# Routing of a mixture of experts rewritten: sums of squares, top two, ranks and block numbers computed in another way

## The chip, the cores and the metric

One core of a Trainium2 chip runs the whole program. The metric is the device time of one execution in microseconds. The core has five engines that run side by side and meet at semaphores: TensorE (matrix products, PE in the profile), VectorE (DVE), ScalarE (ACT), GpSimd (POOL) and SyncE (SP, which here only issues DMAs). Sixteen DMA engines move data between the main memory and the on-chip memory.

## The reference

One layer of a streaming encoder on 544 tokens (512 of a prompt and 32 of a sample), 1024 wide. After the two mixers comes `x = x + merged @ w_out`, and then the part that the change is about:

```python
h2 = rmsnorm(x)
g_prob = softmax(h2 @ w_rg + b_rg)                    # 4 groups
p_top, g_top = top_k(g_prob, 1)
e_logits = (h2 @ w_re + b_re).reshape(n, 4, 8)        # 32 experts
v_top, i_top = top_k(e_logits[arange(n), g_top], 2)
gates = softmax(v_top) * p_top
...                                                   # the tokens are sorted by expert
y[tok] += gate * (silu(xb @ w_gate[e]) * (xb @ w_up[e])) @ w_down[e]
```

Each token goes to two experts of one group. An expert has three weight matrices of 2 MB each in fp32, 192 MB over all.

## The kernel before

All products run in fp32 or in two fp32r parts. The tokens lie in five tiles, four of 128 and one of 32. In the last product of the mixers, "W_o", the result comes out with features on partitions: 8 tiles `yT[:, j, :]` of 128 features by 544 tokens. They are made in a loop over j on TensorE (`product("wo", j)`), ScalarE copies each out of the accumulators, and TensorE adds the tile's part of the router's logits behind the next product (`logits(j)`, L1274, out 64 x 544).

After the last tile TensorE turns the five token tiles back to tokens on partitions (`x2_rows`, L1296), and the logits too (L1304). ScalarE takes squares with a running sum (L1763), a root over all (L1767, which first loads a function table), VectorE copies the rows (L2090) and takes the inverse. Then ScalarE scales the rows into `h2` (L1773) and SyncE stores them to main memory (L777, `rows_stored`).

VectorE does the routing, each step waiting for the one before it (`run` = instruction, then wait): logits scaled and biased (L2100, L2104), the group's maximum and its one-hot (`first_max`, four instructions), all experts outside of the group pushed down, then the largest, its one-hot, the second and its one-hot (L2132 to L2143). `chosen` lets TensorE count with two fp32 products how many earlier tokens chose each expert (L1312, L1313). VectorE sums the totals over the tiles (L2156), finds by comparisons and a scan of five doublings how many blocks of 64 slots each expert needs (L2159 to L2166), the slot of each choice (to L2178), its block by 47 comparisons (L2189, L2190), and one-hots of block and lane (L2192 to L2197), with GpSimd making a part of them (L902, L904). Twenty-five bf16 products turn these into token numbers by slot (L1320 to L1323, `maps_done`). Every expert has one block of 64 slots of its own; overflow blocks are handled in a loop behind the thirtieth expert, that runs only if there are any (`n_more`).

With the first 128 numbers (`gidx`, L2217) GpSimd gathers the rows of the first pair of experts from main memory (L889), TensorE turns them (L1374), VectorE scales them (L2246) and the expert loop begins: up products (L1348, L1350), SiLU and gate, down products (L1364, L1365), a scatter of the results, the next gather. Ahead of it, TensorE spreads the gates of the last two experts over partitions (L1337) and VectorE builds two selection matrices from them (L2233).

The experts' weights lie in three places of three parts each. SyncE issues the loads in a fixed order (`load_expert`, L764): the first two experts' parts but one behind the mixers' last weights, the third's first part after W_o, then the five stores of `h2`, then the second's last part after all rows are turned, and the third's two other parts after `rows_stored`. From there on a part is loaded when the products have read what lies in its place.

Of the kernel before, what the change touches and what calls it, by code (L numbers as in the profile page):

```python
# [20 lines left out]
ALU = mybir.AluOpType  # L21
# [8 lines left out]
P = 128  # L30
# [26 lines left out]

COLS = {}
# [9 lines left out]
for _name, _n in (("ident", P), ("tri16", P), ("causal", P), ("before", P), ("rope", TOK), ("iota4", GROUPS),  # L68
                  ("iota32", NE), ("base", NE), ("steps", 8), ("blocks", NOVER), ("valid", NT), ("lane", P), ("iota_blk", NBLK), ("blk_start", NBLK - 1), ("tok_p", NT), ("tok_i", NT),
                  ("half", 1)):  # L70
    CONST_AT[_name] = (_c, _n)
    _c += _n
# [3 lines left out]
def shape_constants():  # L76
# [20 lines left out]
    put("iota32", np.arange(NE) - 64.0)  # L97
    put("base", np.arange(NE) * float(SLOTS))
    put("steps", np.arange(1, 9) * float(SLOTS))
    put("blocks", np.arange(NOVER) * 1.0)  # L100
    valid = np.ones((P, NT), np.float32)
    valid[DEC:, NT - 1] = 0.0
    put("valid", valid)
    put("lane", r[None, :] % SLOTS)
    put("iota_blk", np.arange(NBLK) * 1.0)
    put("blk_start", np.arange(1, NBLK) * float(SLOTS))
    put("tok_p", (r[:, None] + 1) * valid)
    put("tok_i", np.arange(NT) * float(P) * valid)
    put("half", (r[:, None] >= SLOTS) - 4.0)
# [165 lines left out]
def _build(nc, t, ctx):  # L275
# [30 lines left out]
    khigh = R("khigh", [1, P], BF16)  # L306
    g_mix = R("g_mix", [P, KD])
# [99 lines left out]
    ob_hi = N_("ob_hi", [P, 8, TOK], F32R)  # L407
    sg1 = N_("sg1", [P, TOK])
# [23 lines left out]
    lgT = F_("lgT", [64, TOK])  # L432
# [18 lines left out]
    over_blk = M_("over_blk", [P, 2 * NT, NBLK - 1])  # L451
    is_blk = M_("is_blk", [P, 2 * NT, NBLK])
    q_p = M_("q_p", [P, 2 * NT, NBLK], BF16)
    q_i = M_("q_i", [P, 2 * NT, NBLK], BF16)
    q_c = M_("q_c", [P, NT, NBLK], BF16)
    lanes = M_("lanes", [P, 2 * NT, P], BF16)
    vacant = M_("vacant", [P, NBLK])
# [109 lines left out]
    logits_done = sem("logits_done")  # L567
    lgT_copied = sem("lgT_copied")
# [3 lines left out]
    x2_ready = sem("x2_ready")  # L572
# [8 lines left out]
    blk_ready = sem("blk_ready")  # L581
    onehots_i_ready = sem("onehots_i_ready")
# [57 lines left out]
    r5 = [T_(f"r5_{n}", [P, NT])[:, :] for n in range(4)]  # L640
# [3 lines left out]
    rE = T_("rE", [P, NT, NE])[:, :, :]  # L644
    rT = T_("rT", [P, NT, NE])[:, :, :]
    O1 = T_("O1", [P, NT, NE])[:, :, :]
    O2 = T_("O2", [P, NT, NE])[:, :, :]
    picks = T_("picks", [P, NT, NE])
    rank = T_("rank", [P, NT, NE])[:, :, :]
    base = T_("tile_base", [P, NT + 1, NE])  # L650
    rd = T_("rd", [P, NT])[:, :]
    cum = [T_(f"cum{n}", [P, NE])[:, :] for n in range(2)]
    nb = T_("nb", [P, NE])[:, :]
    nb8 = T_("nb8", [P, NE, 8])[:, :, :]
    nbe = T_("nbe", [1, NOVER, NE])[:, :, :]
    bef = T_("bef", [1, NOVER])[:, :]
# [6 lines left out]
    assert U_.at <= T_.at  # L663
# [184 lines left out]
    def _(pool):  # L848
# [51 lines left out]
        pool.wait_ge(blk_ready, 1)  # L900
        for c in range(2):
            nc.gpsimd.tensor_tensor(q_i[:, c * NT:(c + 1) * NT, :], is_blk[:, c * NT:(c + 1) * NT, :],  # L902
                                    con("tok_i").unsqueeze(2).to_broadcast([P, NT, NBLK]), ALU.mult)
        nc.gpsimd.tensor_tensor(q_c[:, :, :], is_blk[:, NT:, :], con("valid").unsqueeze(2).to_broadcast([P, NT, NBLK]),  # L904
                                ALU.mult).then_inc(onehots_i_ready, 1)
# [49 lines left out]
    def _(pe):  # L955
# [313 lines left out]

        def logits(j):  # L1270

            pe.wait_ge(x2T_read, j + 1)
            for half in range(2):
                mm = pe.matmul(bank[0:64, 2 + half, 0:HALF], w_rt[:, j, :], yT[:, j, half * HALF:(half + 1) * HALF],  # L1274
                               start=(j == 0), stop=(j == KD - 1))
            if j == KD - 1:
                mm.then_inc(logits_done, 1)

        for j in range(8):
            product("wo", j)  # L1280
            if j >= 1:
                logits(j - 1)
        logits(7)

        def x2_rows(i):

            r = ROWS[i]
            if i in (0, 3):
                if i:
                    pe.wait_ge(x2_ready, 1)  # L1290
# [8 lines left out]
        for i in range(3):  # L1299
            x2_rows(i)  # L1300
        pe.wait_ge(lgT_copied, 1)
        for i in range(NT):
            r = ROWS[i]
            mm = pe.transpose(bank[0:r, 2, i * 64:(i + 1) * 64], lgT[:, i * P:i * P + r], ident[0:64, 0:64])  # L1304
        mm.then_inc(lg_done, 1)
        for i in range(3, NT):
            x2_rows(i)

        pe.wait_ge(chosen, 1)
        pe.wait_ge(x2_ready, NT)  # L1310
        Mf = picks[:, :, :].rearrange("p i e -> p (i e)")
        pe.matmul(bank[:, 0, 0:NT * NE], con("before"), Mf, start=True, stop=True)  # L1312
        pe.matmul(bank[:, 1, 0:NT * NE], ones[:, :], Mf, start=True, stop=True).then_inc(ranks_done, 1)  # L1313

        pe.wait_ge(onehots_ready, 2)
        pe.wait_ge(onehots_i_ready, 1)
        at = bank[:, 3, 0:NBLK]
        for n in range(2 * NT):
            pe.matmul(at, lanes[:, n, :], q_p[:, n, :], start=(n == 0), stop=False)  # L1320
            mm = pe.matmul(at, lanes[:, n, :], q_i[:, n, :], start=False, stop=(n == 2 * NT - 1))
        for i in range(NT):
            mm = pe.matmul(bank[:, 2, 0:NBLK], lanes[:, NT + i, :], q_c[:, i, :], start=(i == 0), stop=(i == NT - 1))  # L1323
        mm.then_inc(maps_done, 1)
# [4 lines left out]
        pe.wait_ge(gidx_ready, 1)  # L1329
# [3 lines left out]
        for s in range(2):  # L1333
            row = proj[:, s, :, :].rearrange("p a b -> p (a b)")
            for i in range(NT):
                r = ROWS[i]
                mm = pe.matmul(row[:, i * P:i * P + r], last_gates[0:r, i, s:s + 1].to_broadcast([r, P]), ident[0:r, 0:r],  # L1337
                               start=True, stop=True)
# [60 lines left out]

        turn_rows(16)  # L1400
# [95 lines left out]
    def _(act):  # L1496
# [255 lines left out]
        for j in range(8):  # L1752
# [4 lines left out]
        act.wait_ge(logits_done, 1)  # L1757
        nc.scalar.copy(halves(lgT[:, :]), bank[0:64, 2:4, 0:HALF]).then_inc(lgT_copied, 1)

        for i in range(NT):  # L1760
            r = ROWS[i]
            act.wait_ge(x2_turned, i + 1)
            step(nc.scalar.activation(h2[0:r, i, :].rearrange("p (a b) -> p a b", a=2), x2_source(i)[0:r], ACT.Square,  # L1763
                                      accum_out=st_x[0:r, 1, i:i + 1]))
            step.settle()
            act.sem_inc(x2_squared, 1)
        nc.scalar.activation(st_x[:, 1, :], st_x[:, 1, :], ACT.Sqrt, scale=1.0 / D, bias=eps_col[:, :]).then_inc(x2_rms, 1)  # L1767
        act.wait_ge(x2_inv, 1)
        for i in range(NT):

            r = ROWS[i]
            act.wait_ge(x2_ready, i + 1)
            nc.scalar.mul(h2[0:r, i, :], X[0:r, i, :], st_x[0:r, 4, i:i + 1]).then_inc(h2_ready, 1)  # L1773
# [608 lines left out]
```

## Time and profile before

| what | us |
|---|---|
| median of 3 runs (1191.23 to 1192.43) | 1191.29 |
| the profiled execution | 1190.86 |
| its span in the profile | 1189.0 |
| TensorE busy | 1031.5 |
| VectorE busy | 380.1 |
| ScalarE busy | 281.7 |
| GpSimd busy | 238.7 |

The busy times are sums over the span, and tell nothing of which engine is waited for at a given moment; the last 430 us and the 50 us ahead of them are quite different stages.
### The profile page before, as it was taken

What the parts mean: (1) busy time and instruction counts of PE and PEld (TensorE: products, weight loads), DVE (VectorE), ACT (ScalarE), POOL (GpSimd) and SP (SyncE); (2) the same over time, 40 slices, a digit from 0 to 9 for tenths busy, and PEclk for the clock granted to TensorE, in tenths of its full rate; (3) what the DMA queues carried; (4) which work ended last, traced back from release to release, by engine and by line L of the source; (5) the groups of instructions that cost most, each with busy time, mean ns of one, the idle gap of its engine ahead of it and who ended that gap; (6) DMA issues with size and microseconds to landing.
All of it is one profiled execution on the core that took longest, in us unless ns stands there. A gap on an engine that the chain in (4) does not pass through costs nothing.

```text
span 1189.0 us, 15070 instructions
## 1 busy us (share of the span) xinstructions
PE 1031.5 (87%) x6236; PEld 709.2 (60%) x6236; DVE 380.1 (32%) x715; ACT 281.7 (24%) x449; POOL 238.7 (20%) x134
## 2 busy tenths in 40 slices
PE   3987999999989998999999279998888778888886
PEld 2976787776978887999998143333333333233332
DVE  6067322334357419332100821211111111111117
ACT  5234434336254524222211500000000000000003
POOL 3322112121321226433421011111111100111100
PEclk9988999998999979999999679998888998888898
DMA  7335111110321122343355739999999999999994
GB/s 203 77 89 190 36 36 41 50 36 19 98 54 28 45 63 68 92 130 110 90 226 220 322 115 411 428 427 429 432 429 429 433 429 429 432 429 429 427 416 156
DMA packets 109470, 267.60 MB, mean 225 GB/s; under 512 B 22477, under 2 KB 89325, under 8 KB 96194
## 3 DMA queue, kind: packets, MB, share of 16 engines
q1 hardware_dynamic: 104706, 258.11, 56.2%
q0 software_dynamic: 4704, 8.64, 1.9%
q8 instruction: 45, 0.74, 0.3%
q14 instruction: 15, 0.12, 0.0%
HBM read 256.17 MB, written 18.17 MB: 231 GB/s over the span
## 4 chain that ended last, share of the span: by engine, by line
PE 58%; DMA 24%; DVE 11%; issue 3%; ACT 3%; SPq 0%; DVEq 0%; ACTq 0%
PE proj L999 29%; DMA we<-in_w_exp_up 22%; PE proj L1348 11%; PE proj L1364 3%; PE bank L1091 2%; PE bank L1121 2%; DMA raw<-in_w_in 1%; DVE ors L1829 1%; PE proj L975 1%; PE bank L1108 1%; DVE ex L1994 1%; PE bank L1374 1%; PE bank L1274 1%; PE proj L1237 1%; DVE ex L1977 1%
## 5 line engine op out<-in xcount | busy, mean ns | idle before, releaser
L1348 PE MATMUL proj<-we,xsT 128*64 128x512 f32 x512 | 251.8, 649 | 65.5 <-DMA we<-in_w_exp_up 55.2
L1350 PE MATMUL proj<-we,xsT 128*64 128x512 f32 x512 | 252.1, 650 | 0.0
L855 POOL TENSOR_TENSOR wlo<-raw,whi 128x1024 fp32r<-128x1024 f32 x70 | 162.6, 2324 | 421.0 <-PE proj L999 408.4
L1348 PEld LDWEIGHTS proj<-we,xsT 128*64 128x64 f32 x512 | 73.7, 150 | 211.9 <-issue 198.9
L999 PE MATMUL proj<-hT_hi,whi 128*128 128x272 f32 x704 | 151.3, 297 | 10.7 <-DVE hT_lo L265 8.2
L999 PE MATMUL proj<-hT_hi,wlo 128*128 128x272 f32 x704 | 149.0, 294 | 0.0
L999 PE MATMUL proj<-hT_lo,whi 128*128 128x272 f32 x704 | 148.8, 293 | 0.0
L1505 ACT CAST whi<-raw 128x1024 fp32r<-128x1024 f32 x70 | 69.7, 999 | 223.5 <-PE proj L999 213.7
L1783 ACT ACTIVATE hg<-proj 64x512 f32<-64x512 f32 x30 | 17.7, 590 | 441.2 <-PE proj L1350 441.2
L999 PEld LDWEIGHTS proj<-hT_hi,whi 128*128 128x128 f32 x704 | 113.1, 193 | 15.1 <-DVE hT_lo L265 8.3
L2238 DVE TENSOR_TENSOR hg<-hg,proj 64x512 f32<-64x512 f32 x32 | 22.1, 690 | 308.9 <-ACT hg L1783 293.7
L1364 PE MATMUL proj<-we,hT 128*64 128x512 f32 x256 | 115.2, 592 | 1.1 <-DVE hT L2241 1.1
L1365 PE MATMUL proj<-we,hT 128*64 128x512 f32 x256 | 115.2, 592 | 0.0
L999 PEld LDWEIGHTS proj<-hT_lo,whi 128*128 128x128 f32 x704 | 112.7, 192 | 1.6 <-issue 0.9
L999 PEld LDWEIGHTS proj<-hT_hi,wlo 128*128 128x128 f32 x704 | 112.1, 192 | 1.6 <-issue 0.9
L894 POOL DMA_INDIRECT expert_out<-yo,sidx x30 | 29.8, 995 | 386.5 <-DVE sidx L2258 375.8
L1364 PEld LDWEIGHTS proj<-we,hT 128*64 128x64 f32 x256 | 34.9, 137 | 71.6 <-issue 69.6
L1350 PEld LDWEIGHTS proj<-we,xsT 128*64 128x64 f32 x512 | 73.7, 150 | 0.0
L2255 DVE COPY yo<-proj 128x512 f32<-128x512 f32 x30 | 20.7, 691 | 66.1 <-PE proj L1365 66.1
L1926 DVE TENSOR_REDUCE stat<-bank 128x1 f32<-128x128 f32 (+4 forms) x40 | 19.3, 482 | 63.7 <-PE bank L1095 55.1
L1365 PEld LDWEIGHTS proj<-we,hT 128*64 128x64 f32 x256 | 34.9, 137 | 0.0
L1091 PE MATMUL bank<-kcat,qT 96*128 96x128 f32 (+4 forms) x80 | 31.1, 470 | 0.4 <-ACT kcat L1579 0.4
(334 smaller groups left out, 1425.2 us busy)
## 6 DMA issues: line engine op xcount, KB each, us to landing
we<-in_w_exp_gate SPq DMA_DIRECT2D x31, 2048.0 KB, 31.7
we<-in_w_exp_up SPq DMA_DIRECT2D x31, 2048.0 KB, 36.2
we<-in_w_exp_down SPq DMA_DIRECT2D x31, 2048.0 KB, 38.4
raw<-in_w_in SPq DMA_DIRECT2D x43, 512.0 KB, 3.6
expert_out<-S_smp SPq DMA_DIRECT2D x1, 4352.0 KB, 14.9
x_rows<-in_x_prompt SPq DMA_DIRECT2D x8, 512.0 KB, 4.6
raw<-in_w_branch_b SPq DMA_DIRECT2D x8, 512.0 KB, 3.8
raw<-in_w_out SPq DMA_DIRECT2D x8, 512.0 KB, 3.7
```

Of the source, the lines that this page charges most:

```text
L855: nc.gpsimd.tensor_tensor(lo[:, 0:c], raw[n % NRAW][:, 0:c], hi[:, 0:c].bitcast(F32), ALU.subtract).then_inc(w_split, 1)
L894: pool.indirect_dma_start(out=ys[:, :], out_offset=bass.IndirectOffsetOnAxis(ap=sidx[s][:, 0:1], axis=0), in_=yo[:, s, :], in_offset=None, ...
L999: mm = pe.matmul(proj[:, slot, half, 0:HALF], w[:, at:at + P], r[:, k, half * HALF:(half + 1) * HALF], start=(m == 0), stop=(m == len(term ...
L1091: mm = pe.matmul(bank[0:r, u % 2, 0:n], qT[0:QK, h, q0:q0 + r], kcat[hp % 2][0:QK, a, k0:k0 + n], start=True, stop=(i == 4))
L1121: mm = pe.matmul(bank[64 * a:64 * a + 64, 3, 0:r], V[0:kr_, vb, h * VD:(h + 1) * VD], probT[u % 2][0:kr_, b * r:(b + 1) * r], start=(b == ...
L1348: pe.matmul(proj[0:SLOTS, s, 0, :], xsT[:, k, cols], wg[:, k * FF:(k + 1) * FF], start=(k == 0), stop=(k == KD - 1))
L1350: mm = pe.matmul(proj[64:64 + SLOTS, s, 0, :], xsT[:, k, cols], wu[:, k * FF:(k + 1) * FF], start=(k == 0), stop=(k == KD - 1))
L1364: pe.matmul(proj[0:SLOTS, s, 1, :], hT2[:, s, k, :], wd[:, k * D:k * D + FF], start=(k == 0), stop=(k == 3))
L1365: mm = pe.matmul(proj[64:64 + SLOTS, s, 1, :], hT2[:, s, k, :], wd[:, k * D + FF:(k + 1) * D], start=(k == 0), stop=(k == 3))
L1505: nc.scalar.copy(whi[n % NHIGH][:, 0:c], raw[n % NRAW][:, 0:c]).then_inc(w_high, 1)
L2238: v.tensor_tensor(hg[0:SLOTS, s, :], hg[0:SLOTS, s, :], proj[64:64 + SLOTS, s, 0, :], ALU.mult).then_inc(done, 1)
L2255: v.tensor_copy(yo[:, s, :], proj[:, s, 1, :])
```

## The change

- The sums of squares are no longer taken by ScalarE from the turned rows. VectorE squares each `yT` tile as it comes and adds it to a sum of tiles; TensorE sums over partitions with one column of ones, into a 37th column beside the logits. The logits are computed with the tokens as stationary operand, so that they come out with tokens on partitions and need no turning. The last `yT` tile is copied half by ScalarE, half by VectorE.
- ScalarE asks for a root before the W_o loop. It scales the turned rows from the accumulators into `h2` and copies them to `X` itself.
- The top two come from VectorE's instructions for the eight largest values and their indices, one each per token tile; both one-hots from one comparison.
- Ranks over all tiles and the totals come from eleven bf16 products on TensorE. The fifth tile of rows is turned behind them.
- Block numbers come from adding and subtracting 1.5 x 2^29, where numbers round to multiples of 64, and from one scan instruction. Lanes are one-hots of 64 columns in fp32, token numbers stand in one fp32 operand, GpSimd has no part in it.
- The first `gidx` is read straight from the accumulators. The gates, the table of overflow blocks and the scatter numbers are computed behind it. The gate rows are transposes.

The core of the diff:

```diff
@@ TensorE
+        pe.matmul(bank[:, 2, 0:NT * 64], ident, w_rt[:, 0, NL:NL + 1].to_broadcast([P, NT * 64]), start=True, stop=False)
         def logits(j):
-            for half in range(2):
-                mm = pe.matmul(bank[0:64, 2 + half, 0:HALF], w_rt[:, j, :], yT[:, j, half * HALF:(half + 1) * HALF], ...
+            for i in range(NT):
+                pe.matmul(bank[0:r, 2, i * 64:i * 64 + NL], yT[:, j, i * P:i * P + r], w_rt[:, j, 0:NL],
+                          start=False, stop=False)
+        def squares_sum(src, stop):
+            for i in (4, 0, 1, 2, 3):
+                mm = pe.matmul(bank[0:r, 2, i * 64 + NL:i * 64 + NL + 1], src[:, i * P:i * P + r], ones[:, 0:1], ...
...
+        squares_sum(x_sums, False)
         logits(7)
+        squares_sum(x_squares, True)
-        for i in range(3):
+        for i in range(4):
             x2_rows(i)
...
+        pe.matmul(rank, before_b[:, :], picks[:, :, :].rearrange("p i e -> p (i e)"), start=True, stop=False)
+        for i in range(4):
+            pe.matmul(bank[:, 3, (i + 1) * NE:NT * NE]..., ones_b[:, :], picks[:, i:i + 1, :].to_broadcast([P, 4 - i, NE]), ...
+        pe.matmul(totals, ones_b[0:1, :], shift_b[0:1, :], start=True, stop=False)
+        for i in range(NT):
+            mm = pe.matmul(totals, ones_b[0:r, :], picks[0:r, i, :], start=False, stop=(i == NT - 1))
+        x2_rows(4)
+        def on_lanes(out, n, r, values, start, stop):
+            for half in range(2):
+                rows_ = slice(half * SLOTS, (half + 1) * SLOTS)
+                mm = pe.matmul(out[rows_], lanes[0:r, n, :], values, start=start, stop=stop)
@@ ScalarE
+        nc.scalar.activation(st_x[:, 1, :], st_x[:, 1, :], ACT.Sqrt)
...
+        normed_row(0)
+        plain_row(0)
+        normed_row(1)
+        plain_row(1)
+        for i in range(2, NT):
+            normed_row(i)
+        for i in range(2, NT):
+            plain_row(i)
@@ VectorE
+        for j in range(7):
+            dve.wait_ge(x2T_read, j + 1)
+            run(v.tensor_tensor(x_squares[:, :] if j else x_sums[:, :], yT[:, j, :], yT[:, j, :], ALU.mult))
+            if j:
+                run(v.tensor_tensor(x_sums[:, :], x_sums[:, :], x_squares[:, :], ALU.add))
...
+        for i in range(NT):
+            step(v.max(top[:, i, :], rE[:, i, :]))
+        step.settle()
+        for i in range(NT):
+            step(v.max_index(top_at[:, i, :], top[:, i, :], rE[:, i, :]))
+        step.settle()
+        run(v.tensor_copy(expert[:, :, :], top_at[:, :, 0:2].rearrange("p i c -> p c i")))
+        run(v.tensor_tensor(O, con("iota32")..., expert[:, :, :]..., ALU.is_equal))
+        v.tensor_tensor(picks[:, :, :], O[:, 0], O[:, 1], ALU.add).then_inc(chosen, 1)
...
+        run(v.tensor_scalar(extra, totals, 0.5 - SLOTS / 2, ROUND, ALU.max, ALU.add))
+        run(v.tensor_tensor_scan(starts[:, 1:NE + 1], extra, con("round"), 0.0, ALU.add, ALU.subtract))
+        run(v.tensor_tensor(over, starts[:, 0:NE], con("over_base"), ALU.add))
+        run(v.scalar_tensor_tensor(rT, rank, float(SLOTS), over..., ALU.is_ge, ALU.mult))
+        run(v.tensor_tensor(rT, rT, rank, ALU.add))
+        run(v.tensor_tensor(chosen_rank, O, two(rT), ALU.mult))
+        run(v.tensor_reduce(slotF[:, :, :], chosen_rank, AX.X, ALU.add))
+        run(v.scalar_tensor_tensor(slotF[:, :, :], expert[:, :, :], float(SLOTS), slotF[:, :, :], ALU.mult, ALU.add))
+        run(v.tensor_scalar(blkF[:, :, :], slotF[:, :, :], 0.5 - SLOTS / 2, ROUND, ALU.add, ALU.add))
+        run(v.scalar_tensor_tensor(neg_lane[:, :, :], blkF[:, :, :], ROUND, slotF[:, :, :], ALU.subtract, ALU.subtract))
+        step(v.tensor_tensor(lanes[:, :, :], cross(neg_lane[:, :, :], SLOTS), con("neg_lane")..., ALU.is_equal))
         for c in range(2):
+            for i in range(NT):
+                last = v.tensor_scalar(token_at[:, c * NT + i, :], con("iota_blk"), blkF[:, c, i:i + 1], con("token")[:, i:i + 1],
+                                       ALU.is_equal, ALU.mult)
+            last.then_inc(onehots_ready, 1)
...
         dve.wait_ge(maps_done, 1)
+        for s in range(2):
+            last = v.tensor_scalar(gidx[lane, :], token[lane, s:s + 1], float(VACANT), None, ALU.add)
+        last.then_inc(gidx_ready, 1)
```

## Rows read from the trace of the kernel before

**Rows 1.** Stretches: engines' busy us (instructions), granted clock, DMA share, GB/s.

```profile
680.00:685.00 5.00, 0.00 (x0) 0.00 (x0) 4.90 (x8) 0.00 (x0) 3.31 (x3) 0.50 0.98 419
685.00:690.00 5.00, 2.22 (x30) 2.15 (x31) 3.37 (x15) 0.00 (x0) 1.21 (x1) 0.50 0.03 10
...
760.00:1140.00 380.00, 316.55 (x1406) 123.84 (x1402) 65.27 (x152) 14.76 (x25) 37.34 (x37) 0.91 1.01 429
```

**Rows 2.** Chain that ended last, in order of time: start, us, what.

```profile
1050.60 38.65 DMA we<-in_w_exp_up
```

**Rows 3.** SyncE's queue in order of time: start us, us, what it issued.

```profile
663.40 4.47 SPq L777 DMA_DIRECT2D token_rows<-h  x5
667.92 0.94 SPq L764 DMA_DIRECT2D we<-in_w_exp_down  x1
...
670.99 0.45 SPq L764 DMA_DIRECT2D we<-in_w_exp_down  x1
706.50 0.33 SPq L764 DMA_DIRECT2D we<-in_w_exp_gate  x1
```

**Rows 4.** TensorE, end of W_o, logits and turning: start us, us, operation.

```profile
642.24 1.13 PE L1274 MATMUL bank<-yT,w_rt 128*64 128x272 f32 x4
...
651.14 2.05 PE L1274 MATMUL bank<-yT,w_rt 128*64 128x272 f32 x8
...
653.12 1.09 PE L1296 MATMUL bank<-cst,yT 128*128 128x128 f32 x8
...
655.88 0.52 PE L1304 MATMUL bank<-cst,lgT 64*128 64x64 f32 x5
```

**Rows 5.** ScalarE after W_o: start us, us, operation.

```profile
654.24 1.02 ACT L1763 ACTIVATE h<-bank 128x1024 f32<-128x1024 f32 x1 [0.42 <-PE bank L1296]
...
660.38 1.28 ACT L1767 ACT_TABLE_LOAD   x1
```

**Rows 6.** VectorE through the routing: start us, us, operation.

```profile
662.23 0.40 DVE L2100 TENSOR_TENSOR LG<-bank,st_x 128x144 f32<-128x144 f32 x2
...
664.46 0.33 DVE L2132 TENSOR_TENSOR rE<-LG,rOG 128x160 f32<-128x160 f32 x1
664.82 0.32 DVE L2134 TENSOR_TENSOR rE<-rE,rPen 128x160 f32<-128x160 f32 x1
...
669.83 0.32 DVE L2143 TENSOR_TENSOR picks<-rT,cst 128x160 f32<-128x160 f32 x1
...
671.79 0.09 DVE L2154 MEMSET tile_base<- 128x32 f32 x1 [0.73 <-PE bank L1313]
...
674.51 0.15 DVE L2165 COPY cum<-cum 128x1 f32<-128x1 f32 x1
674.58 0.18 DVE L2166 TENSOR_TENSOR cum<-cum 128x31 f32<-128x31 f32 x1
...
681.53 1.49 DVE L2194 TENSOR_TENSOR lanes<-slotF,cst 128x1280 bf16<-128x1280 f32 x1
```

**Rows 7.** Map products on TensorE, then GpSimd's issue of the gather.

```profile
685.04 0.20 PE L1320 MATMUL bank<-q_p,lanes 128*128 128x48 bf16 x1 [13.39 <-POOL q_c L904]
...
685.82 0.38 PE L1323 MATMUL bank<-q_c,lanes 128*128 128x48 bf16 x5
...
688.37 1.21 POOL L889 DMA_INDIRECT xsb<-token_rows,gidx  x1 [3.48 <-DVE gidx L2217]
```

**Rows 8.** Gather: landing of the first, then of all sixteen.

```profile
DMA to landing us min/median/max: 4.3/4.3/4.3
DMA to landing us min/median/max: 4.1/11.9/12.8
```

**Rows 9.** TensorE from the gate rows to the first up product.

```profile
688.94 5.18 PE L1337 MATMUL proj<-cst,last_gates 128*128 128x128 f32 x20 [2.74 <-DVE last_gates L2228]
694.05 1.97 PE L1374 MATMUL bank<-cst,xsb 128*128 128x128 f32 x8
697.40 1.11 PE L1348 MATMUL proj<-we,xsT 128*64 128x512 f32 x1 [1.38 <-DVE xsT L2246]
```

More of the change, by code:

```diff
@@ L56 @@
 EXP_CAP = 80.0
+ROUND = 1.5 * 2.0 ** 29
+VACANT = 1024
+assert SLOTS == 64 and VACANT >= TOK
 COLS = {}
@@ L96, in shape_constants @@
     put("iota4", np.arange(GROUPS) - 64.0)
[L97 to L109, printed above, removed]
+    put("iota32", np.arange(NE) * 1.0)
+    put("over_base", NMAIN - SLOTS - np.arange(NE) * float(SLOTS))
+    put("round", np.full(NE, ROUND))
+    put("blocks", np.arange(NOVER) * float(SLOTS))
+    put("neg_lane", -1.0 * np.arange(SLOTS))
+    put("iota_blk", ROUND + np.arange(NBLK) * float(SLOTS))
+    put("token", r[:, None] + P * np.arange(NT) - float(VACANT))
+    put("half", 1.0 * (r[:, None] >= SLOTS))
     return c
@@ L450, in _build @@
     blkF = M_("blkF", [P, 2, NT])
[L451 to L457, printed above, removed]
+    neg_lane = M_("neg_lane", [P, 2, NT])
+    token_at = M_("token_at", [P, 2 * NT, NBLK])
+    second_at = M_("second_at", [P, NT, NBLK])
+    lanes = M_("lanes", [P, 2 * NT, SLOTS])
+    SQ = W_.at - 3 * PART
+    x_sums = nc.alloc_sbuf_tensor_at("x_sums", [P, TOK], F32, offset=SQ)
+    x_squares = nc.alloc_sbuf_tensor_at("x_squares", [P, TOK], F32, offset=SQ + TOK * 4)
+    assert SQ >= AFTER_OB - 8 * TOK * 4 and SQ + 2 * TOK * 4 <= AFTER_OB
     assert M_.at <= K_.at
@@ L639, in _build @@
     LG = T_("LG", [P, NT, GROUPS + NE])
-    r5 = [T_(f"r5_{n}", [P, NT])[:, :] for n in range(4)]
+    rE = T_("rE", [P, NT, NE])[:, :, :]
+    rT = T_("rT", [P, NT, NE])[:, :, :]
+    chosen_rank = T_("chosen_rank", [P, 2, NT, NE])[:, :, :, :]
+    picks = T_("picks", [P, NT, NE], BF16)
+    top = T_("top", [P, NT, 8])
+    top_at = T_("top_at", [P, NT, 8], U32)
     rG = T_("rG", [P, NT, GROUPS])[:, :, :]
@@ L643, in _build @@
     rPen = T_("rPen", [P, NT, GROUPS])[:, :, :]
[L644 to L650, printed above, removed]
-    rd = T_("rd", [P, NT])[:, :]
-    cum = [T_(f"cum{n}", [P, NE])[:, :] for n in range(2)]
-    nb = T_("nb", [P, NE])[:, :]
-    nb8 = T_("nb8", [P, NE, 8])[:, :, :]
+    O = T_("O", [P, 2, NT, NE], BF16)[:, :, :, :]
+    r5 = [T_(f"r5_{n}", [P, NT])[:, :] for n in range(3)]
+    rd = T_("rd", [P, NT])[:, :]
+    expert = T_("expert", [P, 2, NT])
+    both_gates = T_("both_gates", [P, 2, NT, 2])[:, :, :, :]
+    extra = T_("extra", [P, NE])[:, :]
+    over = T_("over", [P, NE])[:, :]
+    starts = T_("starts", [P, NE + 1])
     nbe = T_("nbe", [1, NOVER, NE])[:, :, :]
-    bef = T_("bef", [1, NOVER])[:, :]
+    bef = T_("bef", [1, NOVER + 1])
     assert T_.at <= LAST, T_.at
@@ L1302, in _ @@
+        pe.matmul(totals, ones_b[0:1, :], shift_b[0:1, :], start=True, stop=False)
         for i in range(NT):
             r = ROWS[i]
[L1304 to L1312, printed above, removed]
@@ L2022, in new_state @@
             dve.sem_inc(proj_read[o % 2], 1)
+        step(v.tensor_copy(before_b[:, :], con("before")))
         dve.wait_ge(sides_loaded, 96)
@@ L2113, in row, with two @@
             return con(name).unsqueeze(1).to_broadcast([P, NT, n])
-        def run(ins):
-            step(ins)
-            step.settle()
+        def two(ap):
+            return ap.unsqueeze(1).to_broadcast([P, 2, NT, NE])
         def first_max(out, val, m, iota, n):
@@ new lines, in _ @@
+        step.settle()
+        run(v.tensor_copy(expert[:, :, :], top_at[:, :, 0:2].rearrange("p i c -> p c i")))
+        run(v.tensor_tensor(O, con("iota32").unsqueeze(1).unsqueeze(1).to_broadcast([P, 2, NT, NE]),
+                            expert[:, :, :].unsqueeze(3).to_broadcast([P, 2, NT, NE]), ALU.is_equal))
+        v.tensor_tensor(picks[:, :, :], O[:, 0], O[:, 1], ALU.add).then_inc(chosen, 1)
+        v.tensor_tensor(rd, top[:, :, 1], top[:, :, 0], ALU.subtract).then_inc(rt_exp_in, 1)
```

237 lines of the change are left out of this document (103 added, 134 removed).

## The prediction

> **What bounds the kernel now.** I read the stretches first. The 16 DMA engines are the bound from 760 us to 1140 us: share 1.01 at 429 GB/s, while TensorE's busy share is 317 of 380 us [rows 1]. The chain of waits says the same: its long pieces there are transfers of expert weights, 38.65 us for one [rows 2]. So after the routing the time is a fixed amount of weights at a fixed rate, and the end moves one for one with the moment at which that stream starts again. Then I asked where it stands still. The share is 0.98 in 680 to 685 us and 0.03 in 685 to 690 us [rows 1]; SyncE's queue issues the third expert's last part at 670.99 us and the next load at 706.50 us [rows 3]. All three places of weights are full, and the first comes free when the first expert's up products end. That is 21 us in which nothing of the bound resource moves, and what stands there is the routing: TensorE, VectorE, GpSimd's gather and the first up products in a row. What is taken out of this row is won, until something else is last in it.
>
> **The change, in order of time.** "W" is the end of the last W_o product, 651.14 us now.
>
> *Before W.* A block of logits is now 4 passes over 272 columns at 0.27 us, 1.06 us apart in all (1.13 us less the drain) [rows 4]. The new form has 10 passes per block, each with 128 tokens as weights and 36 columns. The nearest row is the five transposes of the logits (64 columns, 128 weight columns), 0.52 us with a drain of 0.22, so 0.075 us each; the upper end is the 128-column transposes, (1.09-0.27)/7 = 0.117 [rows 4]. I take 0.075: a block 0.75 us. Six blocks lie between products: 6 x 0.31 = 1.8 us less. The clearing product of 320 columns adds two passes, 0.6 us. W comes 1.2 us earlier, at 649.9 (bounds: 1.3 us later at 0.117, 2 earlier). VectorE's squares and sums (two passes over 544 columns, about 1.3 us, per 8.9 us product) and the two small copies of constants lie in time in which it is idle.
>
> *W to the first logits on VectorE.* Now 651.14 to 662.23 = 11.1 us: last logits, turning, five squares on ScalarE (654.24 to 660.38, 1.23 us each), the load of a function table 1.28 us, root, inverse [rows 4 to 6]. New: TensorE does logits 6, sums, logits 7, sums: 40 passes x 0.075 = 3.0 us, then root and inverse 0.7 us. The table load goes because a root is asked for early, in idle time, and the functions between are copies and squares, before which no load stands in the trace. 3.7 us, 7.4 us less (5.7 less at 0.117). The turned rows are then scaled and copied by ScalarE beside the routing (six times 1.05 us up to row 3), off the path.
>
> *Logits to "chosen".* Now 662.23 to 670.15 = 7.9 us [rows 6]. Scale and bias become one instruction each: 0.75 us. The group part is untouched, 1.36 us. The 5.7 us from 664.46 to 670.15 (16 steps of 160 columns at 0.36 us) become: one addition 0.36; five "largest eight" and five "index of"; a copy 0.20; a comparison of 320 columns 0.52; a sum 0.33. The eight-largest and its index stand nowhere in the trace. From below: instructions of 32 columns or fewer with no wait between start 0.08 us apart [rows 6], so 10 take 0.9 us; from above: each as dear as a settled 160-column step, 3.6 us. The columns (32) are near the first, but the index looks like more than one pass; I take 1.9. Sum 5.4 us, 2.5 less (0.8 to 3.5).
>
> *Ranks.* 670.15 to 671.79 = 1.64 us [rows 6] with four fp32 passes of 160 columns; the granted clock is 0.50, the 1.2 GHz level, from 680 to 690 us [rows 1], as TensorE had hardly worked since 659, and the same is taken here. New: 11 bf16 matmuls, 672 columns in all, about 0.8 us with the hand-over. 0.8 less. The turning of row 4 now stands behind them on TensorE, 0.95 us, then its scaling and its store. "Rows stored" comes at about 665 us, as the store lands 3 us after its issue; the gather needs it at 668, so this new wait is covered by 3 us.
>
> *VectorE to the one-hots.* 671.79 to TensorE's first map product at 685.04 = 13.25 us [rows 6, 7]. New: clamp 0.21, running sum (not in the trace; 0.2 to 0.4) 0.25, offset 0.22, two of 160 columns 0.72, two of 320 columns 1.04, three of 10 columns 0.60, lanes of 640 instead of 1280 columns 0.72 (1.49 [rows 6] less 640/0.96 ns, less overlap), five of 48 columns at 0.11, 0.65: 4.4 us and 0.1 hand-over. 8.75 less. The second five end 0.6 us later, while TensorE works on the first. The two GpSimd products go, and nothing takes their place.
>
> *Maps to the gather's issue.* 685.04 to 688.37 = 3.33 us [rows 7]: 25 bf16 matmuls 0.04 us apart, VectorE finishing the block table, two steps, indices 0.31, hand-over 0.95. New: 40 fp32 passes of 48 columns. 
>
> The gather is issued 1.2+7.4+2.5+0.8+8.75-0.6 = 20.05 us earlier, at 668.3.
>
> *The gather's landing.* This is where gain is given back. Now it is issued into idle DMA engines and lands after 4.3 us; the median of all 16 gathers, nearly all issued into the stream, is 11.9, the longest 12.8 [rows 8]. Its data are 0.5 MB, so the difference is waiting. Will the engines be idle at 668? The last three loads are tied to the turning and storing of the rows. The first of them moves from 667.9 [rows 3] to about 662, the two others from 671 to 665.4; three loads are 6.29 MB / 429 GB/s = 14.7 us and about 2 us to start, so the engines are full until 679. The gather falls inside, and I take 11.9 us: 680.2. The Trainium skill (DMA: Bandwidth & Descriptors, "Queues, rings and completion order") says that each engine alternates between the queue rows packet by packet; with SyncE's packets larger than a gathered row this agrees with 11.9 against 4.3.
>
> *To the first up product.* Now the rows land at 692.7 but TensorE is on the gate rows until 694.05 [rows 9]: 1.35 us go, as these become 10 one-pass transposes (2.6 us) and end near 672, and VectorE's picks near 674, both before 680. Gate arithmetic and the block table, moved behind the indices, are covered by the gather's flight; in a flight of 4 us they would just be. Turning and scaling stay 3.35 us [rows 9], the first up products 9.1 us (697.40 to 706.50): TensorE has idled in both cases and starts at the 1.2 GHz level.
>
> Sum: 20.05 - 7.6 + 1.35 = 13.8 us. The profiled execution took 1190.86 us (span 1189.0), so 1177.1; its time is 0.4 under the median of the runs, 1191.29, from which it is 1177.5. I say 1177.3.
>
> **The rivals.**
> 1. *The gather is not held up* (the two loads queue behind each other and leave it its turns, or the row stores come so late that they do not run yet). It lands after 4.3 us: 7.6 us more, 1169.7. For: only two loads are outstanding, in the stream more. Against: the median of 16 is 11.9 [rows 8], so waiting in the stream is the rule. 0.17.
> 2. *Small instructions are dearer than their columns*: 0.117 us passes (2.5 + 1.7), index steps 1.7, maps one after the other 2.5: 8.4. All of them together are unlikely and a later issue meets less of the weights' stream (3 us): 5 us less gain, 1182.5. For: each of these has no row of its own. 0.15.
> 3. *The start is earlier but the stream does not gain*, because TensorE, not the DMA engines, sets the pace behind it: within noise, 1191. For: TensorE is busy 83% from 760 to 1140. Against: the share of 1.01 there. 0.02.
> 4. *Slower*: block numbers by rounding give an overflow block that is not there now. The loop for them stands behind the 30th expert and takes one more expert through one set of buffers: gather 4, weights 14.7 (loaded in no shadow), products and store some 12, about 30 us: 1207. It decides from the first count that rounds up; a count of 64 gives 31.5/64, which rounds down, so it would have to be misrounded. 0.02. Dear DVE instructions alone would need 1.4 us more for each of the ten new ones to reach the old time. 0.02.
>
> **The numbers.** Forecast 0.62, the rest as above. A measurement of this kernel tells about 0.2% (2.4 us) from no change. Faster 0.95, same 0.02, slower 0.03. The range goes from just above rival 1 to rival 2: 1170 to 1182.5.
>
> **What would show it.** Issue of the gather at 668 (666 to 673), its landing after 8 to 12 us with the DMA share near 1 around it, first up product at 683 to 684, next weights issued at 693. W at 650; no table load before the root; "eight largest" 0.1 to 0.2 us apart. Wrong if the stream restarts earlier and the end does not follow, or the gather lands in 5 us.

## The result, and the profile after

The changed kernel took 1182.93 us (median of 4 runs, 1182.23 to 1183.09), the kernel before 1191.26 us beside it (1190.25 to 1192.43): a ratio of 0.9929 (0.9911 to 0.9946). So it is 8.3 us faster where 13.8 were forecast, and 0.4 us above the upper end of the range. The profiled execution took 1182.23 us (span 1180.4) against 1190.86 (span 1189.0), a gain of 8.6 us, and the tables below split that.

First the stretches of the kernel after (us from:to, length, then busy us and instructions of TensorE, its weight load, VectorE, ScalarE, GpSimd, then granted clock, DMA share, GB/s):

```profile
675.00:680.00 5.00, 0.40 (x2) 0.18 (x1) 1.29 (x2) 0.00 (x0) 0.00 (x0) 0.50 1.01 428
680.00:685.00 5.00, 1.94 (x8) 1.57 (x8) 0.00 (x0) 0.00 (x0) 0.00 (x0) 0.50 0.53 218
685.00:690.00 5.00, 3.63 (x10) 1.17 (x12) 1.49 (x4) 0.00 (x0) 1.00 (x1) 0.50 0.14 39
690.00:695.00 5.00, 5.00 (x22) 1.53 (x20) 0.00 (x0) 0.00 (x0) 0.00 (x0) 0.83 0.03 11
...
760.00:1130.00 370.00, 306.95 (x1363) 121.93 (x1362) 62.85 (x147) 14.19 (x24) 37.42 (x37) 0.91 1.01 426
```

The hole in the weights' stream [rows 1] is still there, but shorter and elsewhere: the DMA engines are full until about 682.6, and nearly empty until the next load. In the last row stands a number that the prediction had taken as fixed: 426 GB/s where the kernel before has 430 in the same stretch. Next GpSimd's issue of the first gather, and the chain of waits from it on (start us, us, what):

```profile
672.11 1.21 POOL L894 DMA_INDIRECT xsb<-token_rows,gidx  x1 [34.10 <-DVE gidx L2228]
```

```profile
672.11 10.81 DMA xsb<-token_rows,gidx
683.05 1.96 PE bank L1398 x8
685.03 1.30 DVE xsT L2276 x2
686.37 1.11 PE proj L1372
```

The gather is issued at 672.11 instead of 688.37 [rows 7], but it now lands after 10.8 us instead of 4.3 [rows 8]. SyncE's queue shows the reason, which is the one forecast (start us, us, what it issued):

```profile
652.26 0.33 SPq L769 DMA_DIRECT2D we<-in_w_exp_gate  x1
...
658.55 6.73 SPq L782 DMA_DIRECT2D token_rows<-h  x5
665.32 0.43 SPq L769 DMA_DIRECT2D we<-in_w_exp_down  x1
667.27 0.33 SPq L769 DMA_DIRECT2D we<-in_w_exp_up  x1
667.64 0.47 SPq L769 DMA_DIRECT2D we<-in_w_exp_down  x1
696.15 0.33 SPq L769 DMA_DIRECT2D we<-in_w_exp_gate  x1
```

The last three loads are issued 7 to 4.5 us before the gather; before, the last was 17 us ahead of it [rows 3]. The next load comes at 696.15 instead of 706.50, 10.35 us earlier, and of these 1.75 are lost behind it.

TensorE (start us, us, operation; in brackets the idle time ahead and what ended it). The second and third line are the last block of logits that lies between products, and the product behind it:

```profile
582.96 0.70 PE L1271 MATMUL bank<-w_rt,cst 128*128 128x320 f32 x2
...
643.20 1.16 PE L1278 MATMUL bank<-w_rt,yT 128*128 128x36 f32 x10
644.29 0.52 PE L998 MATMUL proj<-mg_hi,whi 128*128 128x272 f32 x2
...
652.07 1.16 PE L1278 MATMUL bank<-w_rt,yT 128*128 128x36 f32 x10
653.06 1.18 PE L1285 MATMUL bank<-ones,x_sums 128*32 128x1 f32 x10
654.11 1.24 PE L1278 MATMUL bank<-w_rt,yT 128*128 128x36 f32 x10
655.19 1.18 PE L1285 MATMUL bank<-ones,x_squares 128*32 128x1 f32 x10
...
661.99 0.24 PE L1321 MATMUL bank<-picks,before_b 128*128 128x160 bf16 x1 [1.42 <-DVE picks L2186]
...
667.89 2.89 PE L1335 MATMUL bank<-token_at,lanes 128*64 128x48 f32 x40 [4.10 <-DVE token_at L2216]
```

ScalarE's root, then VectorE through the routing:

```profile
656.41 0.27 ACT L1793 ACTIVATE st_x<-bank,eps_col 128x5 f32<-128x5 f32 x1 [3.15 <-PE bank L1285]
```

```profile
656.93 0.35 DVE L2168 TENSOR_TENSOR LG<-bank,st_x 128x180 f32<-128x180 f32 x1
...
659.41 0.57 DVE L2178 MAX8 top<-rE 128x8 f32<-128x32 f32 x5
660.01 0.09 DVE L2181 MATCH_VALUE_LOAD top_at<-top,rE 128x8 f32 x1
660.09 0.18 DVE L2181 FIND_INDEX8 top_at<-top,rE 128x8 uint32<-128x32 f32 x1
...
661.69 0.24 DVE L2186 TENSOR_TENSOR picks<-O 128x160 bf16<-128x160 bf16 x1
...
662.84 0.19 DVE L2194 TENSOR_SCALAR extra<-bank 128x32 f32<-128x32 f32 x1 [0.84 <-PE bank L1328]
663.07 0.23 DVE L2195 TENSOR_TENSOR_SCAN starts<-extra,cst 128x32 f32<-128x32 f32 x1
...
666.67 2.23 DVE L2216 TENSOR_SCALAR token_at<-cst,blkF 128x48 f32<-128x48 f32 x10
```

Read as differences between such starts, the two profiled executions give the terms of the sum (us, less is a gain):

| step | forecast | measured | from |
|---|---|---|---|
| start to W | -1.2 | +0.9 | 651.14, 652.07 |
| W to first logits | -7.4 | -6.2 | 11.1, 4.86 |
| logits to "chosen" | -2.5 | -2.9 | 7.9, 5.0 |
| ranks | -0.8 | -0.7 | 1.64, 0.91 |
| to the first map product | -8.75 | -8.2 | 13.25, 5.05 |
| maps to the gather's issue | +0.6 | +0.9 | 3.33, 4.22 |
| issue to turning | +6.25 | +5.3 | 5.68, 10.94 |
| turning to first up product | 0 | 0 | 3.35, 3.32 |
| up product to next loads | 0 | +0.7 | 9.10, 9.78 |
| next loads to the end | 0 | +1.75 | 482.5, 484.25 |
| sum | -13.8 | -8.6 | spans 1189.0, 1180.4 (the rows are rounded) |

### The profile page after: what moved, and what is told of

It reads as the page before. It is cut to its first block and busy times, and to the rows that moved or that the text cites. A ratio compares the mean times of both kernels' runs of the same rounds, so it can differ in the third digit from the quotient of the medians.

```text
span 1180.4 us, 15252 instructions
## 1 busy us (share of the span) xinstructions
PE 1034.0 (88%) x6333; PEld 717.1 (61%) x6333; DVE 380.1 (32%) x709; ACT 280.5 (24%) x445; POOL 235.6 (20%) x131
```

## The experiments

The theory going in, called A, was that of the prediction: the last two loads of weights are in flight when the gather is issued, and these cost it 6 to 7 us. The rival, B, was that something else is late behind the routing (TensorE's clock, or the stream itself), so that a shorter flight of the gather would not reach the end. Below, "W+" is a time counted from W in the same trace, which takes out what happens before. For the changed kernel the gather is issued at W+20.04, the next loads at W+44.08 and the end is at W+528.34; for the kernel before W+37.2, W+55.4 and W+537.9.

**The two loads behind the gather.** `e1_defer`, the changed kernel with

```diff
         sp.wait_ge(rows_stored, 16 * NT)
+        sp.wait_ge(xs_loaded, 16)
         load_expert(2, 1, 2)
```

> The changed kernel, with the third expert's up and down weights loaded only after the first gather has landed (they were issued 4.5 us ahead of it). Theory A (the gather waits for packets of those loads): it lands 4.3 us after its issue instead of 10.9, the first up product starts 6.6 us earlier, the two loads (9.8 us) fit between the landing and the next free place, so the end comes 6.6 us earlier: 1176.3 us. Rival B (the gather is slow for a reason of its own, as the row stores just ahead of it): it lands after 10 to 11 us all the same, the first two experts' products cover the late loads, 1183 us. Rival C (moving 4 MB of the stream to later costs what it saves): landing 4.3, but no gain at the end, 1182 to 1183 us.

Measured: 1174.89 us, ratio 0.9876 (0.986 to 0.9893). GpSimd's issue, the gather's piece in the chain, and the stretch in which the two loads now run:

```profile
671.44 1.21 POOL L895 DMA_INDIRECT xsb<-token_rows,gidx  x1 [34.10 <-DVE gidx L2229]
```

```profile
671.44 4.30 DMA xsb<-token_rows,gidx
```

```profile
680.00:685.00 5.00, 5.00 (x16) 1.47 (x14) 0.00 (x0) 0.00 (x0) 1.00 (x1) 0.59 1.00 428
685.00:690.00 5.00, 3.69 (x18) 0.98 (x14) 0.64 (x1) 0.59 (x1) 0.00 (x0) 1.00 0.76 280
```

The flight falls from 10.8 to 4.3 us with the issue at the same W+20.03; the next loads come at W+37.32, the end at W+521.63, 6.7 us earlier. The two loads run beside the first up products, where the engines stood idle (share 1.00 now), and do not hold up what follows: from the next loads to the end it is 484.3 us in both kernels. So what contention took, it took at the end too.

**TensorE's clock in the flight.** `e2_warm_flight`, the changed kernel with products on constants while the gather flies; their output is not used:

```diff
             mm.then_inc(gate_rows_done, 1)
+        for _ in range(6):
+            pe.matmul(bank[:, 2, :], ident, cst[:, 0:512], start=True, stop=True)
```

> The changed kernel, with 12 passes of 512 columns on TensorE whose result nobody reads, behind the gate rows, while the gather is in flight (from 675.4 to about 683 us). Theory A (the granted clock, low when the gather lands and again for four up products of the second expert, costs time): the turning of rows takes 1.1 us instead of 1.9, the first expert's up products 7.0 instead of 9.8, the second's lose their 1.7 us of slow products; next loads issued 3.6 us earlier, end 3.6 to 5.3 us earlier: 1177.6 to 1179.3 us. Rival B (the stream, not TensorE, sets the time from the start of the experts): the end moves by under 0.5 us, 1183 us.

Measured: 1181.75 us, 0.9918 (0.9895 to 0.994); next loads W+44.40, end W+528.78: nothing gained. The stretches, and the first up product on TensorE:

```profile
680.00:685.00 5.00, 3.02 (x9) 1.23 (x8) 0.00 (x0) 0.00 (x0) 0.00 (x0) 1.00 0.66 275
685.00:690.00 5.00, 3.62 (x16) 1.51 (x17) 1.49 (x4) 0.00 (x0) 1.00 (x1) 0.57 0.00 0
```

```profile
687.33 1.11 PE L1374 MATMUL proj<-we,xsT 128*64 128x512 f32 x1 [1.38 <-DVE xsT L2278]
```

The granted clock did rise to 1.00, the 2.4 GHz level, and the eight turning passes took 1.20 instead of 1.94 us. But the products had ended 2 us before the rows landed, and in the wait for VectorE the clock was at 1.2 GHz again: the first up product takes 1.11 us as before. From the landing to the next loads it is 12.4 us instead of 13.2, but in this run the flight was 1.1 us longer, 12.0 us.

**A delay ahead of the gather.** `e3_delay5`, the changed kernel with 18 steps on VectorE whose results are not used, and `e4_defer_delay5`, the same on top of `e1_defer`:

```diff
         dve.wait_ge(maps_done, 1)
+        for _ in range(18):
+            run(v.tensor_scalar(rE, rE, 1.0, None, ALU.mult))
```

> The changed kernel, with 18 VectorE instructions of 160 columns (4.9 us) before the gather's indices are read. Theory A (the gather lands when the weight loads ahead of it have drained, near 682.5 us, whenever it was issued before): issued at 677, landed at 683.5 to 685, end 0.5 to 2 us later, 1183.5 to 1185 us. Rival B (its flight has a fixed length of 10.9 us): end 4.9 us later, 1187.8 us.

> The deferred loads and the 4.9 us of VectorE instructions together. Theory A: nothing is left that could absorb the delay, 4.9 us more than with the deferred loads alone: 1181.2 us, so below the changed kernel although 4.9 us of work are added. Rival B: 1187.8 us, as with the delay alone.

Measured: 1184.93 us (0.9943, 0.9926 to 0.996) and 1183.11 us (0.9925, 0.9909 to 0.994). In the traces the gather is issued 6.3 and 6.0 us later than without the delay. The delay itself makes 5.0 of these (7.9 us instead of 2.9 from the first map product to the reading of the indices); 1.3 and 0.9 had arisen between W and the first logits, where TensorE's granted clock was lower in these two runs, as in `after_2` below. The gather's piece in the chain of `e3_delay5`:

```profile
683.15 7.61 DMA xsb<-token_rows,gidx
```

With the loads ahead of it the flight shrinks to 7.6 us and the end moves by 3.6 us (W+531.90); with the loads behind it the flight stays at 4.35 us and the end moves by 7.2 us (W+528.84), of which 1.9 arise behind the next loads, for a reason that is not known. So in the changed kernel some four tenths of each microsecond won or lost ahead of the gather are given back in its flight (1 - 3.6/6.3). The pair isn't quite clean: in `e3_delay5` the two loads were also issued later, at W+17.3 instead of W+15.2. Against `after_2`, where they are at W+17.0, the gather is 5.3 us later and the end 2.45, so that rather more than half is given back. The direction holds in both comparisons. This was the reason given in rival 2 for its small instructions costing less at the end than on the engine.

**The same contention in the kernel before.** `e8_before_contended` moves the two loads to just ahead of the gather:

```diff
         sp.wait_ge(rows_stored, 16 * NT)
+        sp.wait_ge(gidx_ready, 1)
         load_expert(2, 1, 2)
```

> The kernel before, with the third expert's up and down weights loaded only when the gather's indices are ready (687.4 us), so that they run beside the gather; everything else, the 21 us of routing too, stays. Theory A (the gather waits for packets of those loads): it lands after 10 to 12 us instead of 4.3; 1.35 us of that is hidden behind the gate rows, so the end comes 4.5 to 6.5 us later, 1195.8 to 1197.8 us. Rival B (the gather in the changed kernel was slow for another reason): it lands after 4 to 5 us, no change, 1191 us.

Measured: 1197.29 us, 1.0067 (1.0046 to 1.0089). SyncE's queue and the gather's piece in the chain:

```profile
687.88 0.33 SPq L764 DMA_DIRECT2D we<-in_w_exp_up  x1
688.26 0.43 SPq L764 DMA_DIRECT2D we<-in_w_exp_down  x1
713.17 0.33 SPq L764 DMA_DIRECT2D we<-in_w_exp_gate  x1
```

```profile
688.77 11.19 DMA xsb<-token_rows,gidx
```

The flight is 11.2 us, the end W+543.3, 5.4 us later than before. The cost is shown from both sides now, with and without the new routing.

**Both kernels again, and the clock with the loads deferred.** `before_2` and `after_2` are the two kernels unchanged; `e7_defer_warm_gap` is `e1_defer` with four products as in `e2_warm_flight` (8 passes, 3.6 us) between the ranks and the maps.

> The kernel before, profiled once more beside the others. In its first profile the weight stream ran at 430 GB/s from 760 us on; in the changed kernel and four variants of it at 425 to 427, which over 182 MB is about 3 us. Theory A (a property of the session, not of the kernel): here it runs at 426 to 427, 1191 us or up to 3 us more. Rival B (a property of the changed kernel): 430 again, and the stretch from the next loads' issue after the routing to the end 482.5 us, as in the first.

> The changed kernel once more. Both theories: 1182 to 1184 us, stream at 426 GB/s, 20.0 us from the end of W_o to the gather's issue, flight 10.9 us.

> The changed kernel with the deferred loads and 8 passes of 512 columns on TensorE between the ranks and the maps, where it idles 4.1 us. Theory A (the granted clock stays up and the small products run at its level): maps and their drain 1.7 us instead of 2.8, rows turned in 1.1 instead of 1.9, first up products 7.0 instead of 9.5, second without its slow products; next loads 3 to 5 us earlier than with the deferred loads alone, end 1170 to 1172 us. Rival B (the clock falls all the same in the gather's flight, or the dummy passes hold up the maps): no gain, 1174 to 1176 us.

Measured: 1191.39 us (1.0001, 0.9991 to 1.0012), 1186.66 us (0.9948, 0.993 to 0.9966), and 1175.69 us (0.9877, 0.9857 to 0.9898). `before_2` repeats itself. `after_2` doesn't quite: 3.7 us over the first set. Its trace has W at 655.39 instead of 652.07 and the gather at W+21.05 instead of W+20.04; from there to the end it is the same within 0.1 us. The 1.0 us behind W is TensorE at the lower clock: the last block of sums takes 2.05 us instead of 1.18, and in the stretch behind it the granted clock is 0.50, the 1.2 GHz level, with TensorE busy all the time. The first trace has 1.00 from 655 to 660 us, where the same work lies:

```profile
658.55 2.05 PE L1285 MATMUL bank<-ones,x_squares 128*32 128x1 f32 x10
```

```profile
660.00:665.00 5.00, 5.00 (x25) 5.00 (x26) 3.69 (x26) 2.76 (x4) 0.00 (x0) 0.50 0.52 215
```

This spread is taken up below. `e7_defer_warm_gap` issues the gather at W+19.15, 0.9 us earlier, and of that 0.4 is left at the end (W+521.20): no gain that can be told. Its first up products start at the 1.2 GHz level all the same (1.11 us each) and take 9.9 us, against 9.5 in `e1_defer`.

**The stream's rate.** What was left was 484.25 us from next loads to the end instead of 482.5, and 426 GB/s instead of 430. In every trace of the new kernel so far it is 426 or 427, in three of the old one (with `e8_before_contended`) 430, so it isn't chance. New buffers and a smaller table of constants stand ahead of the three places of weights, which start at byte 72448 of a partition before (283 x 256) and at 72640 after (192 more). Two theories: the address, or the tail of the new routing. A padding of 64 bytes moves the places to 72704 (284 x 256) in `e9_aligned` and `e10_aligned_defer`, and in the kernel before, where they were aligned, to 72512 (64 more), in `e11_before_shifted`:

```diff
+    pad = R("pad", [P, 16])
```

> The changed kernel with 64 bytes of unused space ahead of the weights' places in SBUF. In three profiles of kernels built on the one before the stream ran at 429 to 430 GB/s, in six built on the changed one at 424 to 427; there the places of the weights start 64 bytes off a multiple of 128 (72640), before at a multiple (72448); with the 64 bytes at 72704. Theory A (the address at which the stream writes sets its rate): 430 GB/s, the stretch from the next loads' issue to the end 482 us instead of 484.2, end 2 us earlier, 1181 us where the changed kernel has 1183. Rival B (something else of the changed program, as the size of its table in main memory): 426 GB/s, no change.

> The 64 bytes and the loads deferred behind the gather. Theory A: both effects add, 7 to 8 us and 2 us under the changed kernel: 1172.5 to 1173.5 us, 430 GB/s. Rival B: as with the deferred loads alone, 1175 us.

> The kernel before with 64 bytes of unused space, so that its places of weights start 64 bytes off a multiple of 128 (72512). Theory A: the rate falls from 430 to 426 GB/s and the stretch from the next loads' issue to the end becomes 2 to 3 us longer (484 to 485 us), 1193.5 us. Rival B: 430 GB/s, 1191.5 us.

Measured: `e9_aligned` 1183.57 us (0.993, 0.9914 to 0.9947; one of its six executions took 2509 us, for an unknown reason, and without it the median is 1183.47), `e10_aligned_defer` 1175.89 us (0.9861, 0.9844 to 0.9879), `e11_before_shifted` 1195.77 us (1.0036, 1.0023 to 1.0049). The long stretch of each, `e9_aligned` and then `e11_before_shifted`:

```profile
760.00:1130.00 370.00, 310.60 (x1382) 123.09 (x1378) 63.92 (x149) 14.17 (x24) 37.31 (x37) 0.92 1.01 429
```

```profile
760.00:1130.00 370.00, 305.56 (x1354) 122.39 (x1352) 61.56 (x144) 14.19 (x24) 36.34 (x36) 0.91 1.01 426
```

From next loads to the end it is 481.63, 481.76 and 484.87 us. The address decides, in both kernels; the old one pays 3.6 us in the median (1195.77 against 1192.13) for 64 bytes. The padding moves all buffers behind it, the gathered rows' too, but the records of single transfers in the traces put the cost on the weights: from 760 to 1130 us their pieces of 16 KB take 611.3 to 611.4 ns each in the six traces with the places at 72448 or 72704, and 615.3 to 615.5 in the eight with 72512 or 72640. The Trainium skill (DMA: Bandwidth & Descriptors, "How a descriptor splits into AXI transactions") says that each transaction has to start at a multiple of 256 bytes, and that where a descriptor (one piece of a transfer) starts off such a multiple, the bytes from the boundary below it are fetched unused and still cost time. It speaks of reads, and the places here are written to, so that no run shows whether this is the reason; but the two fast addresses are multiples of 256 and the two slow ones aren't. Other offsets weren't tried.

In medians the aligned form of the changed kernel does not show its 2.6 us (1183.57 against 1182.93 and 1186.66), since the time ahead of W varies by more. `e12_late_sets` was meant to settle that: `e10_aligned_defer` with the two new constants of VectorE set just ahead of the W_o stage instead of at the start of the program.

```diff
-        v.memset(ones_b[:, :], 1.0)
-        v.memset(shift_b[0:1, :], 0.5 - SLOTS / 2 - 1.0)
...
+        step(v.memset(ones_b[:, :], 1.0))
+        step(v.memset(shift_b[0:1, :], 0.5 - SLOTS / 2 - 1.0))
         step(v.tensor_copy(before_b[:, :], con("before")))
```

> The changed kernel with the loads deferred, the 64 bytes, and the two constants of ones and shifts set just ahead of W_o instead of at the program's start. The end of W_o lay at 650.0 to 651.7 us in four profiles of kernels built on the one before, and in nine built on the changed one four times at 651 to 652.6 and five times at 654 to 657, the difference arising between 86 and 296 us with a lower granted clock. Theory A (the two instructions at the start shift something in that stage): W_o ends at 650 to 652 us and the time is 1172 us with little spread. Rival B (chance, or the layout): W_o ends at either, times from 1172 to 1177 us.

Measured: 1174.34 us, 0.9852 (0.9837 to 0.9868), W at 653.32, between 651.41 of `e1_defer` and 655.39 of `e10_aligned_defer`. It is the fastest in the median, but its interval overlaps those of `e10_aligned_defer` and of `e1_defer` (0.986 to 0.9893), and W did not go back to 651. The cause is open.

## Why the prediction came out as it did

The mechanism was right: the stream starts again earlier, the gather falls into the last loads and gives back much of the gain, and the end follows. The time was 5.6 us too low. Of the profile's 8.6 us against 13.8, by steps:

**"W comes 1.2 us earlier" failed**, by 2.1 us. A block of ten passes lies 1.09 us between two products (643.20 to 644.29), 0.11 us a pass, not 0.075, where the old block took 1.06. So the saving of six blocks was put at 1.8 us and is 0.2 (from the first block to W 53.20 us instead of 53.40), which does not pay for the clearing product (0.54 us where 0.6 was taken). The row of the logits' five turnings was the wrong neighbour: the weight loads of these transposes take 0.14 us in the trace, those of the fp32 products here 0.19, and they come 0.11 us apart whatever passes under them. The products of one column show it best: ten of them take the same 1.0 to 1.1 us as ten of 36. So fewer columns bought nothing. The value was within the bounds given (0.075 to 0.117) and nearer to the upper one. The other 0.57 us stand ahead of the W_o stage already (its first product starts at 582.39 before; the clearing product at 582.96), and there two traces of the unchanged old kernel differ by 1.0.

**"W to the first logits" was mis-sized** for the same reason: four groups of ten passes in 4.2 us instead of 3.0, 4.86 in all instead of 3.7. No function table is loaded ahead of the root, as forecast.

**"Logits to chosen" and "ranks" held**: -2.9 and -0.7. The eight-largest come 0.10 us apart, the index steps 0.16 a pair. So the unknown steps were nearer to the lower bound: ten of them in about 1.5 us where 1.9 was taken (bounds 0.9 and 3.6). Rival 2 had priced them dearer; it was wrong in that term.

**"VectorE to the one-hots" was mis-sized by 0.55 us.** The whole is in ten steps of 48 columns with two per-partition operands: 2.23 us, 0.22 apart, where 0.11 was taken from small steps without such operands. Five of them stand ahead of the first map product. The running sum came at 0.23, as assumed.

**"Maps to the gather's issue" held roughly**, +0.9 for +0.6: 40 passes in 2.89 us, side by side in pairs that start 0.14 us apart in the mean (0.107 in a run, with gaps of 0.24 beside the small fifth tile), where 0.12 was taken. The rival's "one after the other" did not happen.

**"The gather's landing" held.** 10.8 us where 11.9 was taken, 1 us better: it was issued 3.8 us later than forecast, and the loads 1.9, so that it met less of them; `e3_delay5` shows that a later issue shortens the flight. "Rows stored" came in time, and the gate rows ended long before the gather.

**"The first up products 9.1 us" failed by 0.7**: TensorE starts them at 1.2 GHz in both kernels, but the first one at full pace comes 5.7 us behind the start here and 4.2 before. In order, before and after:

```profile
701.57 0.59 PE L1348 MATMUL proj<-we,xsT 128*64 128x512 f32 x1
```

```profile
692.07 0.59 PE L1372 MATMUL proj<-we,xsT 128*64 128x512 f32 x1
```

Why it stays low longer is open. TensorE had idled for 7.65 us ahead of turning the rows here and worked on the gate rows before, and with 5.5 us idle `e8_before_contended` has the same 5.7; but `e7_defer_warm_gap` has 5.8 with only 1.3 us idle. The second pair of products also falls back to 1.2 GHz, and the loads after next come 11.0 us behind the next instead of 9.3. That cost nothing at the end: `e8_before_contended` has the same 11.0 and `before_2` 9.3, and both take 481.6 to 481.7 from next loads to the end. Dummy products did not buy the 0.7 back.

**A term was missing**: "a fixed amount of weights at a fixed rate". The amount is fixed, the rate is not: the new buffers shifted the places off a multiple of 256 bytes, 1.75 us in these two traces (482.5 and 484.25 us; the second trace of the old kernel has 481.7), 2.4 to 3.2 between traces of kernels that differ in the padding alone. Nothing in the prediction asked what a new buffer does to those behind it. Without these 1.75 us the median would be 1181.2 by subtraction, in the range.

So of the 5.2 us missing between the two profiles, 3.8 are a later issue of the gather (2.1 from W, 1.2 from W to the first logits, 0.55 from the one-hots, 0.3 from the maps, less 0.35 won at "chosen" and the ranks), 1.75 the address and 0.7 the clock, and the flight gave 1.0 back. Rival 2 named the nearest time (1182.5), but for reasons that were mostly other ones: only its dearer passes were there. **Open** is the time ahead of W: 650.1 to 651.8 us in the four traces of the old kernel and its variants; in the ten of the new one 651.0 to 652.6 in four and 653.3 to 656.8 in six. In those six the extra time arises between about 260 and 450 us, a part of the kernel that the diff touches little, and it goes with a somewhat lower granted clock there. In the same six the clock falls again behind W, as told of `after_2`: from W to the first logits it is 4.86 us in the four and 5.24 to 6.17 in the six. The stretch from 250 to 450 us in the kernel before, in the first trace after, and in `after_2`:

```profile
250.00:450.00 200.00, 186.47 (x1374) 166.09 (x1374) 92.16 (x155) 90.48 (x123) 50.39 (x23) 0.93 0.19 51
```

```profile
250.00:450.00 200.00, 186.47 (x1373) 165.82 (x1374) 92.06 (x158) 89.92 (x123) 49.90 (x23) 0.93 0.19 51
```

```profile
250.00:450.00 200.00, 186.45 (x1355) 164.65 (x1355) 88.79 (x157) 87.95 (x121) 46.43 (x21) 0.91 0.18 48
```

The clock of the first 90 us, which also varies, is not the reason: it is 0.87 in the first trace after and 0.85 in `after_2`, but 0.96 in `e1_defer` and in `e3_delay5`, the trace with the latest W, and 0.87 in `e8_before_contended`, which is the old kernel. That the lower clock from 260 us on is what makes W late is a reading, not shown, and what lowers it is not known. The medians carry this spread: that of the changed kernel was 1182.93 in one set and 1186.66 in the other.

## What to carry to other kernels

When a stage ahead of a gather becomes shorter, look at what else the earlier start sets free: here two loads, each safe to issue a few us later, cost the gather 6.5 us, and one wait that puts them behind it is worth 6.7 us in the traces (1174.89 against 1182.93 us in the medians), not much less than the 8.3 of the whole rewriting. Don't price a short matmul by its columns: look for a row with the same type and weights, since under 128 x 128 fp32 weights one column cost as much as 36 (0.11 us). After a change in a kernel bound by DMA, compare the GB/s of the long stretch and the start addresses of the buffers, which an added buffer moves.

## What the hardware showed unasked

- 64 or 192 bytes off a multiple of 256 in the start of the weights' places took the stream from 429 or 430 GB/s to 426, 2.4 to 3.2 us of 482, in the same direction in two kernels. Each piece of 16 KB took 4 ns more (615.4 instead of 611.4 in the mean), the same for both offsets.
- A gather of 0.5 MB beside two or three outstanding loads of 2.1 MB each flew 10.8 to 12.0 us in five traces, alone 4.3 to 4.5 in eight.
- fp32 products with 128 x 128 weights come 0.11 us apart at 2.4 GHz, be it 36 columns or one.
- The granted clock fell to the 1.2 GHz level in a stretch in which TensorE was busy all the time (660 to 665 us of `after_2`); another trace of the same kernel did the same work at 1.00, and was 0.9 us sooner at the first logits.
- "Index of the eight largest" over 32 columns is two instructions, 0.16 us a pair; ten steps of 48 columns with two per-partition operands took 0.22 each.
